# First two units of a SwiGLU stage in token rows out of a third weight slot, and three down matmuls moved

## The reference

```python
def swiglu(x, w_gate, w_up, w_down):
    h = jax.nn.silu(x @ w_gate) * (x @ w_up)
    return h @ w_down
...
    for i in range(DEPTH):
        x = post_norm(x, 0.5 * swiglu(x, ffn_w_gate[i, 0], ffn_w_up[i, 0], ffn_w_down[i, 0]), ln_g[i, 0], ln_b[i, 0])
        if i % N_MIXERS == 0:
            mix = pool_mixer(x, pool_w[j], pool_b[j], pool_scale[j])
        else:
            mix = swa_sink_attention(x, cos, sin, attn_w_qkv[j], attn_b_qkv[j], attn_sinks[j], attn_w_o[j], attn_b_o[j])
        x = post_norm(x, mix, ln_g[i, 1], ln_b[i, 1])
        x = post_norm(x, 0.5 * swiglu(x, ffn_w_gate[i, 1], ffn_w_up[i, 1], ffn_w_down[i, 1]), ln_g[i, 2], ln_b[i, 2])
```

## Time and profile before

| | us |
|---|---|
| median of 3 runs (879.33 to 880.9) | 879.35 |
| time of the profiled execution | 879.61 |
| its span, first to last instruction | 877.8 |
| TensorE busy in the span | 850.1 |
| VectorE busy | 561.1 |
| ScalarE busy | 415.5 |
| mean granted TensorE clock, 1 is full | 0.995 |

### The profile page before, as it was taken

The page is one execution under the profiler, slowest core; times in us unless marked ns, Lnnn a source line. Parts: engine busy times, 40 slices in busy tenths (PEclk is TensorE's granted clock), DMA queues, the critical chain, the costliest instruction groups (busy, mean ns, idle before and its releaser), DMA issues.

```text
span 877.8 us, 12580 instructions
## 1 busy us (share of the span) xinstructions
PE 850.1 (97%) x4712; PEld 727.4 (83%) x4712; DVE 561.1 (64%) x782; ACT 415.5 (47%) x654; POOL 25.6 (3%) x51
## 2 busy tenths in 40 slices
PE   7999999996999999999999999999989999999996
PEld 6888888886988888888888888887756988888885
DVE  2765565579655655657665655669787856656556
ACT  2555455432354554543454554554564544545540
POOL 0000000001100000001000000011000000000000
PEclk9999999999999999999999999999999999999998
DMA  9986547282585465563756556554145385565501
GB/s 280 351 295 224 184 155 230 72 266 97 193 295 181 160 226 177 168 223 109 238 197 203 180 191 194 189 192 144 49 139 197 104 301 174 189 200 182 191 1 49
DMA packets 116143, 162.19 MB, mean 185 GB/s; under 512 B 3936, under 2 KB 97632, under 8 KB 116112
## 3 DMA queue, kind: packets, MB, share of 16 engines
q1 hardware_dynamic: 112656, 152.06, 52.1%
q0 software_dynamic: 2496, 9.44, 3.1%
q10 hardware_dynamic: 960, 0.27, 0.1%
HBM read 160.70 MB, written 1.05 MB: 184 GB/s over the span
## 4 chain that ended last, share of the span: by engine, by line
PE 91%; DVE 6%; issue 1%; ACT 1%; DMA 1%; DVEq 0%; SPq 0%
PE ps L1083 28%; PE ps L1081 16%; PE ps L1034 10%; PE ps L1036 10%; PE ps L1035 10%; PE ps L1050 6%; PE ps L1080 4%; PE ps L1062 1%; PE ps L907 1%; PE ps L910 1%; PE ps L1115 1%; PE ps L916 1%; DVE xn L740 1%; DVE stats L746 1%; DMA raw_g<-in_ffn_w_gate 1%
## 5 line engine op out<-in xcount | busy, mean ns | idle before, releaser
L1083 PE MATMUL ps<-xT,g_hi 128*128 128x512 f32 x1064 | 379.3, 396 | 0.0
L1081 PE MATMUL ps<-xT,g_lo 128*128 128x256 f32 x1216 | 314.1, 279 | 0.0
L1081 PEld LDWEIGHTS ps<-xT,g_lo 128*128 128x128 f32 x1216 | 229.2, 188 | 12.8
L1083 PEld LDWEIGHTS ps<-xT,g_hi 128*128 128x128 f32 x1064 | 199.7, 188 | 41.2
L690 DVE TENSOR_TENSOR g_lo<-raw_g,g_hi 128x1024 fp32r<-128x1024 f32 x171 | 208.0, 1222 | 25.0 <-ACT g_hi L434 24.9
L700 DVE TENSOR_TENSOR gu<-ps,gu 128x512 f32<-128x512 f32 x76 | 52.6, 692 | 230.5 <-ACT gu L457 230.5
L434 ACT ACTIVATE g_hi<-raw_g 128x1024 fp32r<-128x1024 f32 x172 | 179.7, 1052 | 8.0 <-PE ps L916 3.7
L457 ACT ACTIVATE gu<-ps 128x512 f32<-128x512 f32 x76 | 45.6, 600 | 283.2 <-PE ps L1083 283.2
L1034 PE MATMUL ps<-d_hi,hT_hi 128*128 128x512 f32 x352 | 137.9, 392 | 0.6 <-DVE hT_lo L710 0.6
L1036 PE MATMUL ps<-d_hi,hT_lo 128*128 128x512 f32 x352 | 137.0, 389 | 0.0
L1035 PE MATMUL ps<-d_lo,hT_hi 128*128 128x512 f32 x352 | 137.0, 389 | 0.0
(11 more groups left out here) (128 smaller groups left out, 628.8 us busy)
## 6 DMA issues: line engine op xcount, KB each, us to landing
...
```

The costliest lines, as they stand in the source:

```text
L1081: last = pe.matmul(bank[:, S:2 * S], w_lo, xT_hi[:, k, :], start=False, stop=False)
L1083: last = pe.matmul(bank, w_hi, xT[:, k, :, :], start=False, stop=k == KT - 1)
```

## The change

Units 0 and 1 of stages 1 to 3 are split like all others, into one of the two slots and a new third slot (EXTRA). `gate_up_tokens` multiplies them together: x is the stationary operand, 128 tokens, and the moving one 512 columns, gate and up of both units; h comes out in token rows and is transposed by TensorE (`h_transposes`) into a bank of which ScalarE and VectorE take hi and lo (`first_units`). Unit 2's gate/up then comes before down of unit 0. In stages 1 and 2 the next two splits (`next_splits`; for stage 2 the first two of QKV) stand in unit 20; behind the pool stage and in the last two attention tasks, directly. xf has no room of its own any more, and b_o, the layer norm scale and offset share buffers, with loads of their own. The residual with b_o is taken between QKV chunks. Last, the right columns of unit 18's second token half are multiplied behind the first half's end.

```diff
+X0 = [g - RAW_UNITS for g in G0]
+X_QKV = G_QKV - RAW_UNITS
+EXTRA = 2
+G_SLOTS = 3
...
+        def g_slot(f, u):
+
+            if f is None:
+                return (0, EXTRA, 1, 0, 1, 0)[u]
+            if f > 0 and u == 1:
+                return EXTRA
+            return (u == 0) * (f > 1) if f > 0 and u < 2 else (u - 1) % 2 if f == 1 else u % 2
+
+        def next_splits(f, u, it):
+
+            if 1 <= u < UNITS - 2:
+                return [(f, u + 2, it)]
+            if f in (1, 2) and u == UNITS - 2:
+                return [(f + 1 if f == 1 else None, v, 0) for v in range(2)]
+            return []
+
+        def hT_bank():
+            return ACC[0][0].rearrange("p (u s) -> p u s", u=2)
+
+        def tokens_bank(t):
+            return ps[:, WORK + 2 + t, :].rearrange("p (u m f) -> p u m f", u=2, m=2)
...
+                if f == 0 and c == 2:
+                    sp.wait_ge(g_used, RAW_UNITS)
+                elif f > 0 or c > 2:
                     sp.wait_ge(g_lo_done, 2 * (X0[f] + 2 * c - 2) + 8 * it)
-                elif f > 0:
-                    sp.wait_ge(g_lo_done, 2 * (X0[f] + 2 * c))
...
+                if f > 0:
+                    for c in range(2):
+                        load_gate_up(f, c)
+                    for c in range(2):
+                        load_down(f, c)
+                load_gate_up(f, 2)
+                load_down(f, 2)
...
+                    gp.dma_start(gb[:, 0, :], b_o[0:1, :].to_broadcast([P, D])).then_inc(b_o_in, 16)
+                    sink(0)
+                    sink(1)
+                    gp.wait_ge(res_done, 4)
+                    load_scale(4)
+                    for i in range(2, len(TASKS)):
+                        sink(i)
+                    gp.wait_ge(oT_ps, len(TASKS))
+                    load_offset(4)
...
+                if i >= len(TASKS) - 2:
+                    if i == len(TASKS) - 2:
+                        act.activation(sm[:, 0, 5, 0:1], mhalf[:, :], ACT.Silu)
+                    g_split(3, i - len(TASKS) + 2)
...
-                    after(act, g_used, (G0[f] + u - 3 if f is not None and u < 4 else G - 1) + 4 * it)
+                    if f is None:
+                        after(act, g_used, G_QKV + (-1, 0, 0, 1, 3, 4)[u])
+                    elif f == 0:
+                        after(act, g_used, 0 if u < 4 else G - 1 + 4 * it)
+                    else:
+                        after(act, g_used, G0[f] + (-1, 0, 0, 2)[u] if u < 4 else G - 1 + 4 * it)
                 for half in halves:
-                    act.activation(g_half(g_hi, X, half), src(G, half), ACT.Copy).then_inc(g_hi_done, 1)
+                    act.activation(g_half(g_hi, g_slot(f, u), half), src(G, half), ACT.Copy).then_inc(g_hi_done, 1)
...
-                ahead = (f, u + 2, it) if 1 <= u < UNITS - 2 else (None, 0) if f == 2 and u == UNITS - 2 else None
+                ahead = next_splits(f, u, it)
                 if u not in DIRECT:
                     low_of(f, u, it)
-                if ahead and u not in DIRECT:
-                    g_split(*ahead, halves=(0,))
+                    for a in ahead[0:1]:
+                        g_split(*a, halves=(0,))
...
                 if u + 1 < UNITS:
                     d_split(D0[f] + u + 1, it)
-
-            def channel_major(e):
+                for a in ahead[1:2]:
+                    g_split(*a)
+
+            def silu_tokens(f, t):
+                act.wait_ge(*((tokens_done, f) if t == 0 else (g_used, G0[f] + 2)))
+                act.activation(gu[:, t, 0, :].rearrange("p (u f) -> p u f", u=2), tokens_bank(t)[:, :, 0, :], ACT.Silu).then_inc(silu_done, 1)
+
+            def first_units(f):
+
+                d_split(D0[f])
+                d_split(D0[f] + 1)
+                silu_tokens(f, 1)
+                g_split(f, 3, halves=(0,))
+                act.wait_ge(hT_ps, 2 * f)
+                slot = D0[f] % D_SLOTS
+                act.activation(hT_hi[:, slot:slot + 2, :], hT_bank(), ACT.Copy).then_inc(h_hi_done, 2)
+                g_split(f, 3, halves=(1,))
+                d_split(D0[f] + 2)
+
+            def channel_major(e, between=None):
...
+                    if t == 0 and between:
+                        between()
+
+            def enter(f):
+
+                def between():
+                    g_split(f, RAW_UNITS)
+                    silu_tokens(f, 0)
+
+                channel_major(FFN_EVENT[f], between)
...
-                    g_split(1, RAW_UNITS)
-                    channel_major(1)
+                    g_split(1, 0)
+                    g_split(1, 1)
+                    enter(1)
...
-                    g_split(None, 1)
...
+            dve.wait_ge(b_o_in, 16)
+            for t in range(TT):
+                chunk(1, t)
+                residual_bias(t, gb[:, 0, :])
...
+                if i >= len(TASKS) - 2:
+                    g_split(3, i - len(TASKS) + 2)
...
                 if u + 1 < UNITS:
                     d_split(D0[f] + u + 1, it)
+                for a in ahead[1:2]:
+                    g_split(*a)
+
+            def h_tokens(f, t):
+                dve.wait_ge(silu_done, UNITS * f + t + 1)
+                dve.tensor_tensor(hf[:, t, :].rearrange("p (u f) -> p u f", u=2), gu[:, t, 0, :].rearrange("p (u f) -> p u f", u=2),
+                                  tokens_bank(t)[:, :, 1, :], ALU.mult).then_inc(hf_done, 1)
+
+            def first_units(f):
+
+                d_split(D0[f])
+                h_tokens(f, 1)
+                d_split(D0[f] + 1)
+                g_split(f, 3, halves=(0,))
+                dve.wait_ge(h_hi_done, UNITS * f + 2)
+                slot = D0[f] % D_SLOTS
+                dve.tensor_tensor(hT_lo[:, slot:slot + 2, :], hT_bank(), hT_hi[:, slot:slot + 2, :].bitcast(f32), ALU.subtract).then_inc(h_lo_done, 2)
+                g_split(f, 3, halves=(1,))
+                d_split(D0[f] + 2)
+
+            def enter(f):
+
+                e = FFN_EVENT[f]
+                layer_norm(e, between=lambda: x_lo(e, 0))
+                x_lo(e, 1)
+                h_tokens(f, 0)
+                g_split(f, RAW_UNITS)
 
...
+                        residual_bias(t, pool_bs)
+                    g_split(1, 0)
+                    g_split(1, 1)
+                    enter(1)
...
-                    g_split(None, 1, halves=(0,))
...
-                    dve.wait_ge(tr_done, 4 * QKV_EVENT + 4)
-                    for t in range(TT):
-                        residual_bias(t, aux[:, 1536:2560])
...
+            def gate_up_tokens(f, t):
+
+                e, first = FFN_EVENT[f], g_slot(f, 0)
+                out_, tok = ps[:, WORK + 2 + t, :], slice(t * P, (t + 1) * P)
+                w_hi, w_lo = (b[:, first:EXTRA + 1:EXTRA - first, :].rearrange("p u (m k f) -> p u m k f", m=2, k=KT) for b in (g_hi, g_lo))
+                if t == 0:
+                    pe.wait_ge(g_lo_done, 2 * (X0[f] + 2))
+                for k in range(KT):
+                    if k % 4 == 0:
+                        pe.wait_ge(x_hi_done, 4 * e + 2 * t + k // 4 + 1)
+                    pe.matmul(out_, xT_hi[:, k, tok], w_hi[:, :, :, k, :], start=k == 0, stop=False)
+                    pe.matmul(out_, xT_hi[:, k, tok], w_lo[:, :, :, k, :], start=False, stop=False)
+                for k in range(KT):
+                    if k % 4 == 0:
+                        pe.wait_ge(x_lo_done, 4 * e + 2 * t + k // 4 + 1)
+                    last = pe.matmul(out_, xT_lo[:, k, tok], w_hi[:, :, :, k, :], start=False, stop=k == KT - 1)
+                if t == 0:
+                    last.then_inc(tokens_done, 1)
+                else:
+                    last.then_inc(g_used, 2)
+
+            def h_transposes(f, t):
+
+                pe.wait_ge(hf_done, UNITS * f + t + 1)
+                for u in range(2):
+                    last = pe.transpose(hT_bank()[:, u, t * P:(t + 1) * P], hf[:, t, u * P:(u + 1) * P], ident)
+                last.then_inc(hT_ps, 1)
...
+                else:
+                    gate_up_tokens(f, 0)
                     transposes(e, 1)
-                    gate_up_raw(f, 1, 0, (1,))
-                    gate_up_raw(f, 0, 1)
-                    gate_up_raw(f, 1, 1)
-                ffn_down(f, 0)
+                    gate_up_tokens(f, 1)
+                    h_transposes(f, 0)
+                    gate_up(f, 2, ms=(0,))
+                    h_transposes(f, 1)
+                    gate_up(f, 2, ms=(1,))
+                    ffn_down(f, 0)
                 with pe.Fori(0, (UNITS - 6) // 4) as it:
                     for u in range(2, 6):
-                        gate_up(f, u, it)
                         ffn_down(f, u - 1, it=it)
+                        gate_up(f, u + 1, it)
...
-                ffn_down(f, last_u, (1,))
+                ffn_down(f, last_u, (1,), hs=(0,))
                 for h in range(2):
                     for u in (last_u + 2, last_u + 3):
                         ffn_down(f, u, (0,), hs=(h,))
                 for h in range(2):
```

(2 more changed lines are left out.)

210 lines of the change are left out of this document (97 added, 113 removed).

## The result

The changed kernel takes 890.74 us (median of 4 runs, 890.34 to 891.38), the kernel before 879.65 us (median of 4, 879.33 to 880.9) beside it: a ratio of 1.0124, 95% interval 1.0106 to 1.0142. It is slower, as forecast, but by 11.1 us where +7.2 were forecast, and 0.2 us above the upper end of the range. The profiled execution took 891.38 us with a span of 889.2 (before: 879.61 and 877.8), so its span grew by 11.4. Two executions further down, one of experiment 5 (1011.92 us) and one of experiment 10 (1053.12 us), ran at a mean granted clock of 0.80 and 0.75, a slower state of the whole execution, and are left out of their medians.

What follows compares the result with a forecast made beforehand. TensorE was taken to bound the kernel (busy 850.1 of 877.8 us), with the last engine deciding at stage borders. Terms: -6.6 + 4.7 + 2.9 + 2.9 - 1.2 + 3.8 + 1.4 - 0.7 = +7.2, so 886.6 us; range 882.0 to 890.5.

Steps and rivals of the forecast that it cites:

- New form: Units 0 and 1 of stages 1 to 3: token-row matmuls gain 2.2 us at each of three borders, -6.6 us.
- Rival 3: Token-row matmuls stream slower because of their four runs, as slow as float32: 892 us; chance 0.06.
- (a): Pool stage into stage 1: four g_lo splits on VectorE ahead of layer norm 1, uncovered, +4.7 us.
- (b): End of stage 1: split queued ahead of unit 21's SiLU delays h_lo, TensorE stands still, +2.9 us.
- (c): End of stage 2 into QKV: same wait, +2.9 us; residual and g_lo wait in QKV go, -1.2 us.
- the clock, put at nothing: Clock fall behind the two 2.9 us waits: nothing in the sum, 1.4 us each kept for the upper end.
- (d): End of attention: table load and splits delay the last task's probabilities from 670.39 to 674.15, +3.8 us.
- (e): End of attention: TensorE's 4.3 us idle time lowers the granted clock, +1.4 us.
- The offset: End of attention: layer norm's offset is fetched only after the last output; a late transfer would add, no size given.
- (f): Behind the last stage: first token half finishes three matmuls earlier, VectorE starts its last norm sooner, -0.7 us.
- Rival 2: Splits start in idle time of ScalarE and VectorE, so the stage-end and attention waits vanish: 875.6 us; chance 0.12.

Runs made afterwards that it cites:

- experiment 5: Changed kernel plus seventeen matmuls into an unread bank, filling TensorE's wait for attention's last probabilities: 888.67 us, ratio 1.0093 to the kernel before.
- experiment 10: Kernel with all repairs (splits moved, offset fetched early) plus thirteen unread matmuls in the pool stage's standstill: 869.52 us, ratio 0.9888 to the kernel before.
- experiment 2: Changed kernel plus twelve matmuls into an unread bank during TensorE's wait for hT_lo, ends of stages 1 and 2: 889.37 us, ratio 1.0112 to the kernel before.
- experiment 4: Changed kernel with pT1 in two other buffers, so layer norm's offset is fetched at attention's start: 890.79 us, ratio 1.0123 to the kernel before.

## Why the prediction was right or wrong

- **New form, -2.2 a border: right.** From T of stage 2 to the end of unit 2 it is 22.65 us, 2.4 less than before (22.8 was forecast). The legs agree: that of stage 2 is +2.78 (wait) + 1.7 (clock, experiment 2) - form = +2.30, so the form gives 2.2; in stage 3 it is 3.03 - 0.64 = 2.4; in stage 1 1.8, since its low clock costs 0.3 us more than before up to the second transposes (8.41 us instead of 8.04; at the full clock 6.94 and 6.87). Rival 3 falls: one matmul takes 0.23 us.
- **(a) +4.7: right** (+4.80), and shown from the other side: with the splits elsewhere T is back at 217.0.
- **(b), (c) the waits, +2.9 each: right** (2.78), with the cause named: without the wait on the count they shrink to 0.90.
- **(b), (c) the clock, put at nothing: the step that failed.** The text placed the waits "between 1.94 us, after which the clock stayed at 1.00, and 3.20", and took nothing for the sum. The value nearer to 2.9 was 3.20, and the fall came both times: 2 x 1.7 = 3.4 us of the 4.2 by which the marks of the profiled executions pass the forecast (3.9 between the medians). Most of the rest is the offset (below). It need not have come: over all profiles the clock fell behind 10 of 12 such waits of 2.78 us, so the sum left out what came five times in six. The upper end kept 1.4 for each where one fall cost 1.7. The Trainium skill's page TensorE: Matmul & The Clock Gate (Part 1), which the prediction weighed there, has idle time bringing the throttled clock back; the traces agree for all waits of 3.1 us and longer, for 10 of 12 of 2.78, for some of 1.8 to 1.9, and not for 0.90. By it the forecast would have been 889.4.
- **(d) +3.8 and the table load of 1.28 us: right** (4.18 of wait, 0.58 of it old). **(e) +1.4: right**, 1.5 (experiment 5).
- **The offset, "a late transfer would add to (d)": left without a price.** In the changed kernel it is 1.2 us on the path: the transfer is asked for just behind two weight loads and lands after 6.9 us. Fetched early (experiment 4) it gave 1.2 us at its place, and falls of the clock took them back; with the fall removed (experiment 5) it lands after 4.4 us and the whole wait is gone.
- **(c) -1.2 in QKV: too small.** The marks of the two profiles give -1.6, and the wait for g_lo there is gone; no experiment takes it alone. **(f) -0.7: right** (-0.64).
- **Rival 2** (splits in idle time, 875.6) was wrong for the change as made, by its own condition. Made so by moving them, it holds and more: 871.7.
